# Attention over shared key tiles: values stationary, two heads' turned probabilities as 256 moving columns, reciprocals turned in place of outputs

## The reference, cut to what matters

```
s = q @ k.T * scale (+ bias or mask)     # 128 x (256 to 640)
p = softmax(s)                           # layer 0: the sink joins the sum
o = p @ v                                # 128 x 64
```

## Time and profile before

| | |
|---|---|
| median of 3 runs | 3742.84 us |
| the profiled execution | 3742.77 us |
| its span, first to last instruction | 3741.0 us |
| what lies around the span | 1.8 us |
| PE (matmul) busy | 3561.9 us, 95% |
| PEld (weight load) busy | 2606.6 us, 70% |
| DVE, ACT, POOL busy | 2040.4, 985.3, 1208.0 us |
| mean granted TensorE clock | 0.973 |

### The profile page before, as it was taken

The page is one execution under the profiler, slowest core; times in us unless marked ns, Lnnn a source line. Parts: engine busy times, 40 slices in busy tenths (PEclk is TensorE's granted clock), DMA queues, the critical chain, the costliest instruction groups (busy, mean ns, idle before and its releaser), DMA issues. The chain is left out here.

```text
span 3741.0 us, 43378 instructions
## 1 busy us (share of the span) xinstructions
PE 3561.9 (95%) x15832; PEld 2606.6 (70%) x15832; DVE 2040.4 (55%) x3466; ACT 985.3 (26%) x2281; POOL 1208.0 (32%) x1175
## 2 busy tenths in 40 slices
PE   6999999999999999999999988899999998889999
PEld 4688655555555966588885566688886565668887
DVE  6475456544543166255545268478864348635654
ACT  2067311000020045111121254332212136422211
POOL 1000022222231023244450007556642005645554
PEclk9999999999999999999999998999999998899999
DMA  6300123333321100244442200034443210012222
GB/s 228 108 28 1 54 71 113 125 112 118 113 86 57 52 12 1 68 158 163 158 150 68 73 10 17 25 122 152 151 159 99 74 42 15 7 62 91 85 88 82
DMA packets 91088, 317.58 MB, mean 85 GB/s; under 512 B 10816, under 2 KB 13152, under 8 KB 90880
## 3 DMA queue, kind: packets, MB, share of 16 engines
q1 hardware_dynamic: 64224, 218.34, 18.0%
q10 hardware_dynamic: 24768, 90.19, 6.6%
q0 software_dynamic: 1888, 6.29, 0.6%
HBM read 312.68 MB, written 2.10 MB: 84 GB/s over the span
## 5 line engine op out<-in xcount | busy, mean ns | idle before, releaser
L1100 PE MATMUL ps<-arena 128*128 128x256 f32 (+1 forms) x3552 | 897.4, 406 | 3.2 <-DVE arena L1936 3.2
L1100 PEld LDWEIGHTS ps<-arena 128*128 128x128 f32 x3552 | 674.5, 190 | 192.7 <-issue 4.9
L609 PE MATMUL ps<-hbuf,ring 128*128 128x512 f32 (+1 forms) x1920 | 750.6, 554 | 30.1 <-ACT hbuf L1465 27.4
L609 PEld LDWEIGHTS ps<-hbuf,ring 128*128 128x128 f32 x1920 | 370.2, 193 | 405.8 <-issue 387.9
L2358 POOL TENSOR_TENSOR arena<-ring,arena 128x512 f32<-128x512 f32 (+1 forms) x132 | 169.7, 1286 | 801.6 <-PE ps L1100 801.6
L1100 PE MATMUL ps<-arena,ring 128*128 128x256 f32 (+1 forms) x1040 | 273.7, 406 | 2.0 <-ACT arena L1395 2.0
L1871 DVE CUSTOM_DVE_ANT_0 aring<-aring,csil,adab 128x1024 f32<-128x1024 f32 x176 | 268.6, 1547 | 1.7
L1100 PEld LDWEIGHTS ps<-arena,ring 128*128 128x128 f32 x1040 | 197.3, 190 | 57.5 <-ACT arena L1395 3.8
L913 PEld LDWEIGHTS ps<-arena 128*128 128x128 f32 x1440 | 176.9, 193 | 84.5 <-ACT arena L1290 60.8
L913 PE MATMUL ps<-arena 128*128 128x128 f32 x1440 | 206.5, 288 | 19.3 <-ACT arena L1304 11.9
L2341 POOL TENSOR_TENSOR arena<-ring 128x512 f32<-128x512 f32 (+1 forms) x132 | 169.6, 1285 | 166.6 <-PE ps L1100 164.2
(11 more groups left out here) (272 smaller groups left out, 5074.1 us busy)
## 6 DMA issues: line engine op xcount, KB each, us to landing
aring<-in_ada ACTq DMA_DIRECT2D x172, 512.0 KB, 4.6
ring<-in_mlp SPq DMA_DIRECT2D x128, 512.0 KB, 3.7
ring<-in_up SPq DMA_DIRECT2D x88, 512.0 KB, 3.3
ring<-in_in SPq DMA_DIRECT2D x56, 512.0 KB, 3.2
ring<-in_down SPq DMA_DIRECT2D x32, 512.0 KB, 3.5
ring<-in_odd_in SPq DMA_DIRECT2D x24, 512.0 KB, 3.2
arena<-in_ada SPq DMA_DIRECT2D x16, 512.0 KB, 13.7
ring<-in_out SPq DMA_DIRECT2D x16, 512.0 KB, 3.2
```

The source lines that it names most:

```text
L609: mm = nc.tensor.matmul(slot[:, lo:hi], ring[:, c % RING, k, :], src[:, kt, lo:hi], start=kt == k0, stop=kt == k0 + nkt - 1)
L1100: mm = nc.tensor.matmul(ps[:, bank, 0:tw], w, x, start=start and j == 0, stop=j == len(pairs) - 1, skip_group_check=True)
```

## The change

1. Items are reordered so that two neighbours are the same query block of head h and of head h + 4 (layer 0), which read different key heads but the same value tile of 128 columns. In layers 2 and 3 neighbours already were the two heads of one block.
2. `values` is replaced (outside layer 1) by `pair_values`: on every odd step, the value tile is stationary and the turned probabilities of two items move as 256 columns; the output comes out already turned (feature by token). Four turned-probability buffers take the place of two.
3. `take_o` and `turn_y` go. The reciprocal is written 64 columns wide (the one sum read 64 times), two items side by side; PE transposes that block, ACT copies it to SBUF (`take_inv`), and DVE multiplies the output in PSUM by it, 64 rows at a time, into the activations.
4. Since the heads' order within the activations is another, the rows of the weight `out0` are permuted as they are loaded: four DMAs of 512-byte runs in place of one for each of its 8 chunks. The semaphore counts of the ring follow (`ARRIVED`).

Core of the diff:

```diff
@@ attention_items
-        return ([("a", h, n) for n in range(4) for h in range(8)] + [("b", h, m) for m in range(4) for h in range(8)]
-                + [("ca", h, n) for n in range(2) for h in range(8)] + [("cb", h, n) for n in range(2) for h in range(8)])
+        return [(kind, h + 4 * kv, n) for kind, tiles in (("a", 4), ("b", 4), ("ca", 2), ("cb", 2))
+                for n in range(tiles) for h in range(4) for kv in range(2)]
@@ SP, chunk
+                if name == "out0":
+                    for e in range(2):
+                        for odd in range(2):
+                            to = ring[64 * e:64 * e + 64, c % RING].rearrange("p (g i o) f -> p g i o f", g=2, o=2)[:, :, :, odd]
+                            rows_ = a[name][nb, 64 * odd:64 * odd + 64].rearrange("p (g e i) f -> p g e i f", g=2, e=2)[:, :, e]
+                            sp.dma_start(to, rows_).then_inc(w_arrived[c % RING], 16)
+                    return
@@ PE, attention
+                def pair_values(y):
+                    j = 2 * y + 1
+                    nt = key_tiles(vals[j])
+                    vt = pieces(layer, vals[j])[2]
+                    pe.wait_ge(inv_ready, base + j + 1)
+                    if y >= 1:
+                        pe.wait_ge(yt_taken, ybase + y)
+                    nc.tensor.transpose(ps[:, Y_BANK, (y % 2) * P:(y % 2 + 1) * P], INVS[layer // 2][:, y % 2, :], ident[:, :]).then_inc(yt_ready, 1)
                     pe.wait_ge(pt_copied_act, vbase + j + 1)
                     if nt > 4:
                         pe.wait_ge(pt_copied_dve, p2 + seconds[j])
                     for t in range(nt):
-                        mm = nc.tensor.matmul(ps[:, O_BANK, (j % 2) * P:(j % 2 + 1) * P], pt[:, j % 2, t * P:(t + 1) * P],
-                                              vt[t], start=t == 0, stop=t == nt - 1)
+                        mm = nc.tensor.matmul(ps[:, O_BANK, (y % 2) * 2 * P:(y % 2 + 1) * 2 * P], vt[t],
+                                              turned_pair(layer, y, t), start=t == 0, stop=t == nt - 1)
                     mm.then_inc(o_ready, 1)
@@ PE, the step
                     if j < nv:
                         for i in range(per * j, per * j + per):
                             scores(i)
-                    if 2 <= j <= nv + 1:
-                        values(j - 2)
-                    if j >= 2 + per and j - 2 - per in ys:
-                        turn_y(ys[j - 2 - per])
+                    if layer == 1:
+                        if 2 <= j <= nv + 1:
+                            values(j - 2)
+                        if j >= 4:
+                            turn_y(j - 4)
+                    elif j >= 3 and j % 2:
+                        pair_values((j - 3) // 2)
                     if 1 <= j <= nv:
                         turn(j - 1)
@@ ACT, the step
+                def take_inv(y):
+                    act.wait_ge(yt_ready, ybase + y + 1)
+                    if y >= 2:
+                        act.wait_ge(yt_taken, ybase + y - 1)
+                    nc.scalar.activation((YT, YT2)[layer // 2][:, y % 2, :], ps[:, Y_BANK, (y % 2) * P:(y % 2 + 1) * P],
+                                         ACT.Copy).then_inc(inv_spread, 1)
-                    if j >= 2:
-                        take_o(j - 2)
+                    if j >= 3 and j % 2:
+                        take_inv((j - 3) // 2)
                     if 1 <= j <= nv:
                         copy_pt(j - 1)
@@ DVE, inverse and take_y
                     else:
+                        if layer != 1:
+                            inv, l = INVS[layer // 2][:, i // 2 % 2, 64 * (i % 2):64 * (i % 2) + 64], l.broadcast_to([P, 64])
                         nc.vector.reciprocal(inv, l).then_inc(inv_ready, 1)
...
+                    dve.wait_ge(o_ready, ybase + y + 1)
+                    dve.wait_ge(inv_spread, ybase + y + 1 - len(value_items(1)) * (layer > 1))
+                    for hx in range(2):
+                        rows = slice(64 * hx, 64 * hx + 64)
+                        at = (2 * (y % 2) + hx) * P
+                        o, inv = ps[rows, O_BANK, at:at + P], (YT, YT2)[layer // 2][rows, y % 2, :]
+                        to = dst[rows]
                         if len(dst.shape) == 3:
-                            src = src.rearrange("p (r c) -> p r c", c=16)
-                        nc.vector.tensor_copy(dst, src).then_inc(yt_taken, 1)
+                            o, inv = (v.rearrange("p (r c) -> p r c", c=16) for v in (o, inv))
+                        x = nc.vector.tensor_tensor(to, o, inv, ALU.mult)
+                    x.then_inc(yt_taken, 1)
```

More of the change, by code:

```diff
@@ L720, in stretches @@
             return [(max(lo, a_), min(hi, b_), s_) for a_, b_, s_ in ranges(cols) if max(lo, a_) < min(hi, b_)]
+        ARRIVED = []
+        for c, (name, *_) in enumerate(CHUNKS):
+            ARRIVED.append((ARRIVED[c - RING] if c >= RING else 0) + 16 * (4 if name == "out0" else 1))
         CHUNK_OF = {}
@@ L795, in y_target, with turned, turned_pair @@
             return H[:, 2 + h // 2, n * P:(n + 1) * P]
[L797 to L798 removed]
+        def turned(layer, j):
+            if layer == 0:
+                return PT0[:, j % 4, :]
+            if layer == 1:
+                return PT[:, j % 2, :]
+            return (PT2, JUNK.rearrange("p (s t) -> p s t", s=2))[j // 2 % 2][:, j % 2, :]
+        def turned_pair(layer, y, t):
+            two = (PT0[:, 2 * (y % 2):2 * (y % 2) + 2] if layer == 0
+                   else (PT2, JUNK.rearrange("p (s t) -> p s t", s=2))[y % 2])
+            return two[:, :, t * P:(t + 1) * P]
         def pair_index(blk, d, hx, j):
@@ L903, in values @@
                     nt = key_tiles(vals[j])
-                    vt = pieces(layer, vals[j] if layer != 1 else vals[j])[2]
+                    vt = pieces(layer, vals[j])[2]
+                    pe.wait_ge(pt_copied_act, vbase + j + 1)
+                    pe.wait_ge(pt_copied_dve, p2 + seconds[j])
+                    if j >= 1:
+                        pe.wait_ge(y_ready, j)
+                    for t in range(nt):
+                        mm = nc.tensor.matmul(ps[:, O_BANK, (j % 2) * P:(j % 2 + 1) * P], turned(layer, j)[:, t * P:(t + 1) * P],
+                                              vt[t], start=t == 0, stop=t == nt - 1)
+                    mm.then_inc(o_ready, 1)
+                def pair_values(y):
+                    j = 2 * y + 1
+                    nt = key_tiles(vals[j])
+                    vt = pieces(layer, vals[j])[2]
+                    pe.wait_ge(inv_ready, base + j + 1)
+                    if y >= 1:
+                        pe.wait_ge(yt_taken, ybase + y)
+                    nc.tensor.transpose(ps[:, Y_BANK, (y % 2) * P:(y % 2 + 1) * P], INVS[layer // 2][:, y % 2, :], ident[:, :]).then_inc(yt_ready, 1)
                     pe.wait_ge(pt_copied_act, vbase + j + 1)
@@ L1105, in p1 @@
                     p, x, t, f0, f1 = halves(m)
-                    pe.wait_ge(w_arrived[p.first % RING], 16 * (p.first // RING + 1))
+                    pe.wait_ge(w_arrived[p.first % RING], ARRIVED[p.first])
                     if m >= 2:
@@ L1832, in attention @@
                     conv_center(layer - 2)
-                for j in range(nv + 2 + per):
+                for j in range(nv + (4 if layer == 1 else 2)):
                     if layer >= 2 and j in (1, 6, 7, 14, 15):
@@ L1851, in attention @@
                         copy_pt(j - 1)
-                    if j >= 2 + per and j - 2 - per in ys:
-                        take_y(ys[j - 2 - per])
+                    if layer == 1 and j >= 4:
+                        take_y(j - 4)
+                    if layer != 1 and j >= 3 and j % 2:
+                        take_y((j - 3) // 2)
             def modulate(share):
@@ L2336, in weight_sums @@
                     if which == 0:
-                        pool.wait_ge(w_arrived[(p.first + 1) % RING], 16 * ((p.first + 1) // RING + 1))
+                        pool.wait_ge(w_arrived[(p.first + 1) % RING], ARRIVED[p.first + 1])
                         if n:
```

68 lines of the change are left out of this document (32 added, 36 removed).

## The result

The changed kernel takes **3789.82 us** (median of 4 runs, 3788.39 to 3792.99), the kernel before 3741.75 (3736.18 to 3743.73) beside it: a ratio of 1.0132, 95% interval 1.0115 to 1.0150. The forecast was 3783.6 in a range of 3768 to 3808. The profiled execution took 3790.68 us with a span of 3788.9, where before had 3741.0: 47.9 us more.

A forecast was written before the change was run, and what follows sets the result against it. PE was taken as nearly always streaming in attention, ACT's chain covered with 0.38 us margin. Pair growths 7.7 + 5.4 + 1.9 + 1.8 + 13.9 + 10.1 = 40.8 on 3742.8 gave 3783.6 us, range 3768 to 3808.

The forecast's parts named there:

- The values' gain: Value matmuls on PE: 8 of 256 columns replace 16 of 128 per pair, 1.72 us against 1.96.
- b: Kind of 4-tile attention items in layer 0, 16 pairs: pair from 4.67 to 5.15 us, +7.7 in all.
- The third saved by the estimate: Skill page's matmul spacing, 162 ns against 109: some 39 us off the value instructions, result near 3750; prediction's rows disagreed.
- The step's order: Even steps: only 0.86 us of scores, not 1.84, cover ACT's 1.46 us copy and exponential before `turn`; the costly part.
- restart and slow first transposes: PE restarting on the exponential's signal: 0.06 us, and four transposes 0.06 longer; 0.12 for both.
- a5: Layer 0 kind with five tiles, 8 pairs: values wait for DVE's copy; bounds 6.31 and 7.02 us, upper taken, +10.1.
- `take_inv`, `out0`, the new sequence: ACT's reciprocal copies, `out0` loads in four DMAs (0 to 2 us, taken as 0) and item reordering: no cost.
- the rival: Attention phases: new PE gaps lower the granted clock to 0.87, +50 us, to 3834 us; chance 0.09.
- in kinds b, ca, cb and e DVE has the slack: DVE in these attention kinds: wider reciprocals and two multiplies add nothing, since the pair has just grown.
- ca: Attention kind in layer 0, 8 pairs: pair from 3.10 to 3.34 us, +1.9 in all.
- cb: Attention kind in layer 0, 8 pairs: pair from 2.92 to 3.15 us, +1.8 in all.
- 24 equal pairs of e: Attention of layers 2 and 3: each pair from 4.68 to 5.26 us with a chain of 1.57, +13.9 in all.

The follow-up runs named there:

- Experiment 3: Changed kernel with each value matmul of 256 moving columns made two of 128: 3796.02 us, ratio 1.0152 to the kernel before.
- Experiment 1: Changed kernel with the pair's value matmuls split, half on the odd step and half on the even step after, multiply one step later: 3770.75 us, ratio 1.0070.
- experiments 5 and 6: A one-column ACT exponential added ahead of each exponential in 80 items: on the changed kernel 3788.82 us, on the kernel before 3740.24 us.
- experiment 8: Changed kernel with values split over both steps, multiplies right behind the maximum, reciprocals transposed behind the second half of the values: 3748.26 us, ratio 1.0028.
- the kernel before with the dose: Kernel before with a one-column ACT exponential added ahead of each exponential in 80 items: 3740.24 us, ratio 0.9997.
- Experiment 2: Changed kernel with the transpose of the reciprocals put behind the pair's value matmuls instead of ahead of them: 3797.22 us, ratio 1.0159.

## Why the prediction was right

- **The values' gain is small.** Forecast 0.07 of pitch and two late loads of 0.08 in a pair; measured 1.73 for eight of 256 where two times 0.98 stood. Experiment 3 gives the pitch alone: 0.06 in b. The third saved by the estimate (the Trainium skill, "TensorE: Matmul & The Clock Gate", "Back-to-back issue gap") has no support in this kernel: taking the wide operand away again cost 0.06 of 5.15 us in a pair of b, some 4 us in all.
- **The step's order is the loss.** The chain of copy and exponential was 1.47 against 1.46, and restart and slow first transposes together about the 0.12 assumed. The time before `turn` was forecast at some 0.7 from the scores' end and is 330.12 - 328.60 - 0.86 = 0.66. Experiment 1 (cover back, waits for the exponential a third of what they were) and experiments 5 and 6 (in kind b added ACT time is paid in full after, not at all before) show that this is the cause and not only a fit.
- **a5** took its upper bound, by the path that was worked out, 7.08 against 7.02.
- **`take_inv`, `out0`, the new sequence**: nothing, as taken. (The `out0` phase took 83.9 us in the changed kernel, 1.7 more, and its first 3.4 us, from 433.1 to 436.5, ran at half the clock, which is worth that.) `take_inv` costs nothing where it stands; one experiment further, in the kernel of experiment 8 its copy was on the path to the next values.
- **Clock.** In layer 0 1.00 through the steady stretches, as said, so the rival falls in its own terms: PE is idle for half a microsecond every 5.15 us, 13% of the window 320 to 400, and the clock did not fall. The Trainium skill, "TensorE: Matmul & The Clock Gate", "A second HAM failure mode: psum-queue depth-cycling", describes short idling between groups as what makes the clock go back and forth; these gaps did not. Where the clock did fall is the start of a layer, after a stretch in which PE was busy 1.88 of 5 us (3085 to 3090): 0.50, so 1.2 GHz, the lower of the two levels, from 3090 to 3094. The first pair of layer 3 took 9.96 where the same pair in layer 2 took 7.11, so this cost 2.8 us; a fall in layer 2's second pair (0.57 from 2208 to 2212) cost 11.14 - 9.84 = 1.3. So a sign that the prediction names for being wrong, a granted clock below 1.00 within the phases, did appear, though only in their first two pairs and not by the gaps that its rival meant. It is not shown to be the change's doing. The profiled kernel before has 1.00 in layer 3 after the same idle time (1.89 of 5 us), but the kernel before with the dose, and the one with the four loads, took 9.04 and 9.09 for that first pair instead of 6.24, with 0.50 in their windows. And the profiled kernel before had 0.50 at the start of layer 0: its first pair took 7.19, and 4.62 in those two runs, so 2.6 us; the changed kernel lost 1.1 there (6.53, and 5.44 in the dose's run). With the clock's part taken out on both sides (4.1 + 1.1 after, 2.6 before), the 47.4 us are 44.8, of which layer 0 has 27.7 and layers 2 and 3 have 17.1. That is the change's own cost, and the forecast of 40.8 was 4.0 too low.

- **The step that was off** is the sentence that "in kinds b, ca, cb and e DVE has the slack", and with it the formula's 24 equal pairs of e. For b, ca and cb it holds. In a plain pair of e DVE costs 0.18, of which the forecast missed 0.07, since its chain of 1.57 was 0.10 too long (b's 1.47 is found in e as well). In the four pairs with bias work it is 1.1 us instead of 0.58, 2.1 us in all. In the opening pairs DVE's 512-column reciprocal and the scaling behind it, 3.35 + 1.29, come between the scores and the reciprocal that the values now need: without the clock's part they grew by 18.25 - 1.3 - 14.84 = 2.1 us a layer where 1.2 was forecast, 1.9 more in both. Experiment 2, whose values don't wait for that reciprocal, bears this out: 6.30 + 9.11, only 0.6 above before. Together 1.1 (plain pairs) + 2.1 + 1.9 and the clock's 4.1, less 2.0 at the layers' ends, are the 7.2 us between 13.9 and 21.2. In layer 0 four kinds were 0.03 to 0.06 low; that this doesn't show in its total is luck, since the kernel before had lost 2.6 us to the clock there.

In the opening of layer 3 the reader sees it at once (L2209 and L2211 are the normalisation's work on DVE):

```profile
3100.96 3.35 DVE L2209 RECIPROCAL rstd<-rstd 128x512 f32<-128x512 f32 x1
...
3104.35 1.29 DVE L2211 TENSOR_TENSOR arena<-arena,rstd 128x512 f32<-128x512 f32 x2
...
3107.62 0.33 PE L954 MATMUL ps<-ident,arena 128*128 128x128 f32 x1 [3.05 <-DVE arena L1843]
```

## What to carry to other kernels

When two steps' work on the busy engine is put into one, ask what the other step still covers: read the slower engines' chain from release to signal (here 1.46 us) against what stands between the two ends in each step (1.84, then 0.86). Halving the group instead of alternating it gets the cover back, but the buffers' release and every helper operation (reciprocal, its transpose, its copy, the multiply) then have to be placed one by one, and each has a spot where it costs nothing and one where it costs 0.1 to 0.3 us a pair. Before any of this, price the gain by a row of the same column count: 0.215 against 2 x 0.112 says that there is little to win.

## What the runs showed of the hardware

- In float32 a matmul instruction of 128 moving columns takes 0.112 us of PE from start to start and one of 256 takes 0.215: two narrow for one wide cost 0.06 us in a pair of b (1.79 for 1.73), not more.
- A reciprocal on DVE costs by the column: 158 ns at one, 548 at 64, 6.2 ns for each more. Spreading one column to 64 by a copy takes 196 ns, so computing narrow and copying wide is 0.2 us cheaper.
- A one-column ACT instruction that lasts 0.19 us in the trace delays the next only by 0.09: durations of short ones overlap, and a dose has to be read from starts.
- A wait that ends just as PE needs the operand still costs some 0.15 us, 0.08 before the first matmul of the group and 0.07 to 0.08 on its first loads, though no idle time is listed at PE's matmuls, and 0.28 at its weight loader, put down to issue. A small independent PE instruction in front (here the transpose, 0.11) hides it, in kind b (experiment 2 against the changed kernel).
